# Streaming encoder step on one Trainium2 core: low parts of the expert rows v formed on GpSimd, weighted additions spread over the down stage

## What is computed

```python
def one(xb):
    q = (xb @ w_query).reshape(T, PEER_HEADS, 2, PEER_DKEY // 2)
    s = jnp.einsum('thpd,phkd->thpk', q, sub_keys)
    sv_, si = lax.top_k(s, PEER_TOPK)
    ...
    top_s, pos = lax.top_k(cand, PEER_TOPK)
    idx = jnp.take_along_axis(cand_idx, pos, axis=-1)
    g = jax.nn.softmax(top_s, axis=-1)
    u = expert_u[idx]
    act = jax.nn.gelu(jnp.einsum('td,thkd->thk', xb, u))
    return jnp.einsum('thk,thkd->td', g * act, expert_v[idx])
```

## Time and profile before

| | |
|---|---|
| median of 3 runs | 2036.45 us (2032.37 to 2037.72) |
| the profiled execution's own time | 2028.22 us |
| its span | 2026.4 us |
| PE busy | 1903.6 us (94%) |
| DVE busy | 1365.2 us (67%) |
| ACT busy | 767.3 us (38%) |
| POOL busy | 443.8 us (22%) |
| granted TensorE clock, mean | 0.973 |

### The profile page before, as it was taken

How to read it: one execution, slowest core, us unless ns; L and a number is a source line. 1 busy time by engine, 2 the same in 40 slices (tenths; PEclk the granted TensorE clock), 3 DMA queues, 4 the chain that set the end, 5 groups by cost and what they waited for, 6 DMA issues and landing times.

```text
span 2026.4 us, 28422 instructions
## 1 busy us (share of the span) xinstructions
PE 1903.6 (94%) x11158; PEld 1716.8 (85%) x11158; DVE 1365.2 (67%) x2416; ACT 767.3 (38%) x1046; POOL 443.8 (22%) x377
## 2 busy tenths in 40 slices
PE   7999988897999999999799979999899999999996
PEld 2799975697999999999799969999888888888875
DVE  4433364435359986889877897886467777777776
ACT  1222254412125454544355434554343333333332
POOL 0111100001111472334622354335201111111000
PEclk9999999888999999999899989999999999999998
DMA  7544331031115898988988988999967877777642
GB/s 279 197 149 142 107 133 52 1 105 63 63 44 168 293 377 271 313 297 301 346 283 287 310 292 324 313 319 398 375 231 261 304 266 294 277 284 288 234 176 94
DMA packets 187608, 471.65 MB, mean 233 GB/s; under 512 B 11900, under 2 KB 79064, under 8 KB 183256
## 3 DMA queue, kind: packets, MB, share of 16 engines
q1 hardware_dynamic: 141400, 302.11, 42.5%
q0 software_dynamic: 46080, 167.79, 22.9%
HBM read 414.54 MB, written 55.31 MB: 232 GB/s over the span
## 4 chain that ended last, share of the span: by engine, by line
PE 77%; DVE 13%; DMA 5%; issue 2%; ACT 2%; POOL 1%; SPq 0%; DVEq 0%; ACTq 0%
PE PS L989 26%; PE PS L539 11%; PE PS L541 11%; PE PS L540 11%; PE PS L937 4%; PE PS L603 4%; PE PS L911 2%; DMA gat<-in_peer_v_dram,idx 2%; DVE gat L1746 2%; PE PS L564 1%; POOL gat L1404 1%; DMA G<-gates_dram 1%; DMA gat<-in_peer_u_dram,idx 1%; PE PS L857 1%; PE PS L574 1%
## 5 line engine op out<-in xcount | busy, mean ns | idle before, releaser
L539 PE MATMUL PS<-XH,uth 128*128 128x384 f32 x1024 | 358.5, 350 | 0.0
L540 PE MATMUL PS<-XL,uth 128*128 128x384 f32 x1024 | 346.2, 338 | 0.0
L541 PE MATMUL PS<-XH,utl 128*128 128x384 f32 x1024 | 345.3, 337 | 0.0
L1404 POOL DMA_INDIRECT gat<-in_peer_v_dram,idx x160 | 177.9, 1112 | 562.3 <-DVE acc L1767 503.7
L1404 POOL DMA_INDIRECT gat<-in_peer_u_dram,idx x160 | 206.5, 1291 | 359.1 <-DVE a L1746 287.4
L1880 DVE TENSOR_TENSOR vl<-vrw,vh 128x1024 fp32r<-128x1024 f32 x128 | 156.7, 1224 | 150.5 <-ACT vh L1292 150.5
L1292 ACT ACTIVATE vh<-vrw 128x1024 fp32r<-128x1024 f32 x128 | 135.6, 1060 | 317.3 <-PE PS L989 305.8
L989 PE MATMUL PS<-vh,wh 128*128 128x512 f32 x768 | 243.6, 399 | 8.3 <-DVE vl L1880 5.5
L539 PE MATMUL PS<-XH,whi 128*128 128x272 f32 x784 | 230.9, 295 | 14.9 <-DVE XL L1690 8.2
L989 PE MATMUL PS<-vh,wl 128*128 128x512 f32 x768 | 241.9, 396 | 0.0
L989 PE MATMUL PS<-vl,wh 128*128 128x512 f32 x768 | 240.1, 394 | 0.0
(11 more groups left out here) (284 smaller groups left out, 3188.4 us busy)
## 6 DMA issues: line engine op xcount, KB each, us to landing
uraw<-in_peer_u_dram SPq DMA_DIRECT2D x128, 512.0 KB
vrw<-in_peer_v_dram SPq DMA_DIRECT2D x64, 1024.0 KB, 5.0
acts_dram<-gel SPq DMA_DIRECT2D x128, 192.0 KB
gates_dram<-gst SPq DMA_DIRECT2D x24, 1024.0 KB
al<-acts_dram SPq DMA_DIRECT2D x16, 1536.0 KB, 8.7
G<-gates_dram SPq DMA_DIRECT2D x16, 1536.0 KB, 13.2
adaw<-in_w_ada_dram SPq DMA_DIRECT2D x8, 2048.0 KB, 8.0
wraw<-in_w_in_dram SPq DMA_DIRECT2D x7, 2048.0 KB, 7.8
```

What stands on the lines that cost most here:

```text
L539: mm(out, ah, bh, start=start, stop=False)
L540: mm(out, ah, bl, start=False, stop=False)
L541: return mm(out, al, bh, start=False, stop=stop)
L1404: nc.gpsimd.indirect_dma_start(out=gat[:, n % NGAT, :], out_offset=None, in_=table, in_offset=bass.IndirectOffsetOnAxis(ap=idx[:, k:k + 1] ...
```

## The change

It does four things. The low part vl of each tile of v is subtracted by GpSimd (`v_lo`) instead of DVE; GpSimd does one subtraction and one fetch in turn. DVE does 66 of the 160 weighted additions in the up stage (`IN_UP`) instead of 104, and in the down stage one per tile for tiles 0 to 93 instead of one on every other tile for tiles 0 to 110. ACT and PE turn to the choices at later up tiles, and the fifth token tile's choice has one filler per step instead of two. SP issues the first loads of the down stage at up tile 122 instead of 125.

```diff
--- before.py
+++ after.py
@@ -55,15 +55,16 @@
 
 ORDER = ((3 * P, P), (TP, TS), (0, P), (P, P), (2 * P, P))
 SCORES = (0, 4, 5, 9, 13, 17)
-EXP_AT = (2, 6, 20, 56, 87)
-SEL_AT = (0, 0, 28, 62, 95)
-GATE_AT = (0, 0, 30, 64, 97)
+EXP_AT = (2, 8, 22, 57, 94)
+SEL_AT = (0, 0, 28, 65, 102)
+GATE_AT = (0, 0, 30, 67, 103)
 GATE_PER = (0, 0, 2, 2, 2)
-SCORE_AT = (0, 0, 6, 40, 72)
-GELU_AT = 84
-FILL = (0, 0, 2, 2, 2)
+SCORE_AT = (0, 0, 6, 40, 76)
+GELU_AT = 89
+FILL = (0, 0, 2, 2, 1)
 FILL_HOT = (0, 0, 1, 1, 1)
-EARLY = 36
+EARLY = 20
+IN_UP = 66
 
 
 C_ID, C_TRI, C_MASK, C_MIN, C_IOTA, C_KDEC = 0, 128, 256, 384, 512, 640
@@ -508,7 +509,7 @@
             while stored < NBLK and gate_done(4 * stored + 3) < m - 1:
                 gate_store(stored)
                 stored += 1
-            if m == NU - 3:
+            if m == NU - 6:
                 v_load(0)
                 v_load(1)
                 block_load(0)
@@ -1405,13 +1406,37 @@
                                          in_offset=bass.IndirectOffsetOnAxis(ap=idx[:, k:k + 1], axis=0)
                                          ).then_inc(s_gat[n % NGAT], 16)
 
-        for side, table in enumerate((peer_u[0], peer_v[0])):
-            pool.wait_ge(s_idx, 1)
-            for k in range(P):
-                fetch(NSP * side + k, table, idx3, k)
-            pool.wait_ge(s_idx, 2)
-            for k in range(TS):
-                fetch(NSP * side + P + k, table, idx4, k)
+        def v_lo(j):
+
+            pool.wait_ge(s_vh, j + 1)
+            if j >= 2:
+                pool.wait_ge(s_om, j - 1)
+            else:
+                pool.wait_ge(s_oh, ND * NG)
+                pool.wait_ge(s_gout[0], 16 * (NBLK // 2))
+                pool.wait_ge(s_gout[1], 16 * (NBLK // 2))
+            nc.gpsimd.tensor_tensor(vl[j % 2][:], vrw[:, j // 2 % 2, j % 2, :], f(vh[:, j % 2]), ALU.subtract
+                                    ).then_inc(s_vl, 1)
+
+        pool.wait_ge(s_idx, 1)
+        for k in range(P):
+            fetch(k, peer_u[0], idx3, k)
+        pool.wait_ge(s_idx, 2)
+        for k in range(TS):
+            fetch(P + k, peer_u[0], idx4, k)
+
+        def fetch_v(k):
+
+            if k < NSP:
+                fetch(NSP + k, peer_v[0], idx3 if k < P else idx4, k % P)
+
+        done = IN_UP + NGAT - 1
+        for k in range(done):
+            fetch_v(k)
+        for j in range(NU):
+            v_lo(j)
+            fetch_v(done)
+            done += 1
 
 
     @block.vector
@@ -1863,6 +1888,7 @@
             one_hot(i)
         fill(NSP - dots[0])
         fill(EARLY)
+        assert adds[0] == IN_UP
 
 
         def weights(j):
@@ -1876,8 +1902,6 @@
             tt(wv[:, j % 2], al[:, c % 2, j % JB, :], G[c % 2][:, :, j % JB], ALU.mult).then_inc(s_wv, 1)
 
         def low_parts(j):
-            dve.wait_ge(s_vh, j + 1)
-            tt(vl[j % 2][:], vrw[:, j // 2 % 2, j % 2, :], f(vh[:, j % 2]), ALU.subtract).then_inc(s_vl, 1)
             dve.wait_ge(s_wh, j + 1)
             tt(wl[:, j % 2], wv[:, j % 2], f(wh[:, j % 2]), ALU.subtract).then_inc(s_wl, 1)
 
@@ -1917,8 +1941,7 @@
 
         for j in range(NU):
             weights(j)
-            if j % 2 == 0:
-                weigh()
+            weigh()
             low_parts(j)
             if j == NU - 16:
                 residual(0)
```

## The result

The changed kernel takes **2084.31 us** (median of 4 runs, 2080.84 to 2087.54) against 2034.41 us for the kernel before, run in turn with it: a ratio of **1.0256**, 95% interval 1.0236 to 1.0276. The forecast was 2043.5 us in 2007 to 2070: right in sign, wrong in size, outside its range.

What follows compares the result with a forecast made beforehand. The prediction took TensorE to bound the down stage at 4.17 us per tile, with some 35 us of waits in the up stage; -26 us before the down stage and +33 in it gave +7 on 2036.45, 2043.5 us, range 2007 to 2070.

Steps and rivals of the forecast that it cites:

- The mechanism of the down stage: Down stage: DVE's 2.48 us and GpSimd's 2.08 us add up to 4.56 against 4.17 per tile with an addition, +33 us.
- the cast of the earlier trace: A GpSimd cast of 128 x 1024: 1.04 us alone, 2.10 us when started just behind a two-SBUF-input DVE subtraction.
- I take two passes, 2.08 us: Down stage: GpSimd's subtraction priced as two passes at the cast's rate, 2.08 us, between 1.04 and 3.1 us.
- The end (residuals and output) doesn't change: Last down tiles, with residuals and output: no change in time, 0 us.
- The 34 tiles without an addition: Down stage: 3.7 us plus some 0.3 of signals per tile, under 4.17, so no cost.
- The stalls of the up stage: Up stage: later positions remove PE waits of 15.1, 12.0 and 3.1 us and some 2 us behind them, -32 us.
- no gain there: Up tile 8: the 2.7 us wait for uth stays, as ACT waits there for DVE's sample choice in any case.
- I take 12 us: Hand-over: u is late behind the down stage's earlier loads by 12 us, between 4 and 24.
- The wait at the first down tile: Hand-over: PE's 5.5 us wait at the first down tile goes, since the loads have landed by then.
- Positions and hand-over together: First two stages: -32 us from positions and +6 from the hand-over, -26 us, ends -34 and -14.
- rival 2: Down stage: a dearer subtraction, 2.6 us, costs 78 us, about +52 net, 2088 us; decides from about 2.4 us; chance 0.15.
- rival 3: Up stage: stalls only move, or u holds PE 24 us; gain 10 us instead of 26, 2060 us; chance 0.10.

Runs made afterwards that it cites:

- e1: The changed kernel with the subtraction of vl back on DVE, nothing else: 2023.3 us, 0.9958 of the kernel before.
- e2: The changed kernel with additions from down tile 12 on reading their old sum from PSUM, the accumulation left out: 2061.99 us, single run.
- e6: The changed kernel with down tiles 112 to 127 subtracted on DVE: 2072.07 us, one run.
- e3: The changed kernel with the exponential of the sample tokens' choice back at up tile 6 instead of 8: 2077.51 us, one run.
- e4: The changed kernel with the first loads of the down stage back at up tile 125: 2068.96 us, one run.

## Why the prediction was wrong in size

- **The mechanism of the down stage was right.** Adding DVE's operations and POOL's subtraction up, instead of taking the longest, is what the cast of the earlier trace rows taught, and e1 and e2 show it: without the subtraction on POOL, or without the additions' second SBUF input, the median tile falls from 4.70 to 4.17 and 4.40 us. The waits named (PE for vl or wl) are there, 74 of them.
- **The step that failed is "I take two passes, 2.08 us".** A two-input subtraction of 128 x 1024 on POOL measured 2.40. With 2.40 the prediction's own sum is 2.48 + 2.40 = 4.88 us per tile, 0.71 over 4.17, times 86 = 61 us; measured +54.2 for tiles 11 to 94 and +2.9 ahead of them. The median tile is 4.70 us, the mean 400.3 / 83 = 4.82. Of the 54, (4.70 - 4.17) x 83 = 44 are the typical tile; the other 10 are a net sum: 21 tiles take 5.0 to 5.8 us, 17 of them with a vl of 4.5 to 4.6 us (POOL was passed over, below) and four where ACT waited for v, and most long tiles are followed by one of 4.3. The cast's time was the wrong basis: two reads of one stream each were priced as two casts, and every tenth of a microsecond counted 86 times. The prediction had a better price next to it: from the 4497 ns of the Trainium skill's GPSIMD Engine Reference (Performance versus the Vector engine) it estimated 2.25 us and +48. The measurement is dearer than both. The range was cut too narrow as well: the bounds of 1.04 and 3.1 us gave 0 to +121, and the forecast kept +17 to +48.
- **"The end (residuals and output) doesn't change" failed: +12.9 us** (e6), 8.5 of it where the clock is granted as before. Only the tiles with additions were asked whether they had room. The residuals are DVE operations with two SBUF inputs as well, and the path from ACT's vh to PE had lost its slack.
- **The 34 tiles without an addition** were costed at 3.7 us plus 0.3 and so at nothing; they take 4.18 and 4.42 in turn, +2.5 us for 94 to 112.
- **The stalls of the up stage went about as forecast, their sum partly by luck:** -32 said, -33.1 by the start of uth at up tile 120. By uth's starts the three stalls gave 14.9 (the third choice), 16.9 (the exp at 87) and 2.3 us (the turn at 95), 34.1 together. The rest cancels: a run that is 3.7 us ahead by up tile 29 and a wait for u at tile 117, 3.4 us, that doesn't come back, neither of them forecast, against one loss that no step had, 8.1 us by tile 31. That loss is the sample tokens' choice: DVE waits 8.2 us for its exponential at tile 8, so the choice behind it (index 2) is late, and PE waits 6.3 us at tile 28 (e3 gets 6.9 back). The prediction looked at tile 8 for ACT's wait alone ("no gain there") and not for who waits for the exponential.
- **"I take 12 us" for u behind the hand-over loads** measured 26.0 (uth's starts, up tiles 122 to 127), just past the high end of 24. PE waited 21.0 of them; the other 5 are the granted clock, which fell to the 1.2 GHz level at each of the two waits (0.79 of full speed on average from 1382 to 1440 us, in the last row). These are the rows:

```profile
1387.03 0.98 SPq L481 DMA_DIRECT2D vrw<-in_peer_v_dram  x2
1388.12 0.70 SPq L490 DMA_DIRECT2D al<-acts_dram  x1
1391.18 0.34 SPq L497 DMA_DIRECT2D G<-gates_dram  x1
1395.57 0.33 SPq L465 DMA_DIRECT2D uraw<-in_peer_u_dram  x1
```

```profile
1395.57 26.25 DMA uraw<-in_peer_u_dram
```

```profile
1382.00:1440.00 58.00, 37.04 (x197) 35.77 (x196) 19.21 (x16) 14.68 (x18) 14.28 (x13) 0.79 0.78 308
```

  The load of u issued at 1395.57 lands 26.25 us later (the chain of waits), and from 1376 to 1402 us gathers moved 5.96 MB beside 4.57 MB of SP's: they didn't run out half-way, and SP's queue got 176 GB/s, against the 140 from which the high end was worked out. The wait at the first down tile went as said (-5.3). e4 gets 15.4 us back. Positions and hand-over together gave -12.4 instead of -26.
- **The rivals.** The time came out next to rival 2 (2088 us, from "about 2.4 us on"), and that is in part luck: its point of decision was met, its sum wasn't the one that was paid. It had +78 for the tiles with an addition, where 57 were measured up to tile 94, nothing for the end, and the full -26 ahead of the down stage. There rival 3's other condition came true as well, u that holds PE 24 us: 26.0, and -12.4 instead of -26. The two rivals were priced one at a time, and both happened. Rival 2's 0.15 was too little: the high end of the bound, 3.1 us, and the value taken lay on either side of 2.4.

## What to carry to other kernels

Busy shares do not say whether work may move from DVE to POOL: where both read two inputs from SBUF, add their times up per tile and compare the sum with the bound, and count the residuals and other rare operations too. Where a path is repeated a hundred times, a price that no row has should keep its whole range in the forecast: here 0.3 us was 28 us of the answer. A load that is moved ahead of others delays whatever then stands behind it; look for the consumer with the least slack (u here). The best version (0.983) puts the subtraction, the exponential and the loads back and leaves out one gather and its addition where a block load is on its way.

## What the runs showed that was not expected

- POOL's turn is not given in the order of the records' starts. The Trainium skill's SBUF — State Buffer (SBUF: two separate sides) has it that, of a DVE instruction with two SBUF inputs and a GpSimd instruction that reads SBUF, whichever starts first gets the shared ports for the whole instruction, and the other blocks. The trace agrees that one blocks: DVE's 3.42 and 3.65 us above are 2.1 to 2.7 longer than alone. Which one it is doesn't follow from the starts. A vl that stood ready at 1592.82 us let two DVE operations pass that came after it, and took 4.49 us; and the wv of 3.65 us starts at 1598.78, 0.46 us ahead of the vl that it gives way to. A record's start may not be the moment in which the ports are taken; why POOL is passed over at one operation and let in at the next, no run shows.
- Issuing a gather on POOL seems to get longer beside DVE's operations too: 1.77 us at 1597.45, with an addition and wl on DVE, where a fetch with DVE idle takes 0.94 (at 1462.23 in the kernel before). The mean is 1.30 against 1.11 before. No run tried it by itself.
- Nearly doubling the gathers (20.6 to 38.3 MB in 330 us, e1) took the median v load from 4.9 to 7.1 us, but only one load in four was late enough to show, the one behind a block's al and G.
